# Samples' value pages summed by TensorE in strips of 32 columns, in batches of eight, instead of by VectorE

## The reference, cut to what matters

```
v_past = v_pool[page_table].reshape(db, past, HA, DVA)      # 8 samples x 2048 positions x 4 heads x 128
a = p[:, :, 0] - lam * p[:, :, 1]                           # weights of the two softmax maps
out = einsum('bhqk,bkhe->bqhe', a, v)                       # one query per sample
```

## Time and profile before

| | |
|---|---|
| time, median of 3 | 2703.87 us (2702.91 to 2704.54) |
| the profiled execution's own time | 2701.74 us, of which the span of the trace is 2699.8 us |
| TensorE busy | 2622.1 us, 97% of the span |
| VectorE busy | 1614.7 us, 60% |
| ScalarE, GpSimd busy | 1142.6 us, 1346.6 us |
| chunk loop | 572.30 to 770.13 us of the span |
| output projection | 766.82 to about 897 us |

### The profile page before, as it was taken

The page is one execution under the profiler, slowest core; times in us unless marked ns, Lnnn a source line. Parts: engine busy times, 40 slices in busy tenths (PEclk is TensorE's granted clock), DMA queues, the critical chain, the costliest instruction groups (busy, mean ns, idle before and its releaser), DMA issues.

```text
span 2699.8 us, 46857 instructions
## 1 busy us (share of the span) xinstructions
PE 2622.1 (97%) x17069; PEld 2408.8 (89%) x17069; DVE 1614.7 (60%) x3290; ACT 1142.6 (42%) x1771; POOL 1346.6 (50%) x613
## 2 busy tenths in 40 slices
PE   8999999978899999999999999999999999999998
PEld 5886666667766899999999999999999999999998
DVE  4227768889977343333337885378863788634323
ACT  2228739954423343334333434344343433444433
POOL 0210015610000666667666676676766767666663
PEclk9999999988899999999999999999999999999999
DMA  5220057634585444444444444454444444444553
GB/s 182 68 95 9 17 173 222 195 103 133 155 251 156 134 143 141 137 139 138 139 140 141 134 140 130 138 147 133 140 132 144 132 142 140 134 132 141 149 156 95
DMA packets 457194, 369.01 MB, mean 137 GB/s; under 512 B 15501, under 2 KB 400114, under 8 KB 456732
## 3 DMA queue, kind: packets, MB, share of 16 engines
q1 hardware_dynamic: 444846, 347.05, 43.6%
q0 software_dynamic: 2992, 12.26, 1.5%
q10 hardware_dynamic: 9174, 7.22, 0.9%
HBM read 351.17 MB, written 17.14 MB: 136 GB/s over the span
## 4 chain that ended last, share of the span: by engine, by line
PE 67%; DVE 2%; ACT 1%; issue 1%; DMA 0%; SPq 0%; POOL 0%; DVEq 0%; ACTq 0%
PE bank L2867 21%; PE bank L2869 21%; PE bank L2868 21%; PE bank L2359 3%; DVE tmp L2735 1%; DVE bank L3448 1%; ACT tmp L2727 1%; DMA big<-in_cache_attn_v 0%; PE bank L2743 0%; PE bank L3651 0%; PE bank L2379 0%; SPq L1128 0%; DVE hh L3405 0%; DVE hl L3406 0%; PE bank L1759 0%
## 5 line engine op out<-in xcount | busy, mean ns | idle before, releaser
L3326 POOL TENSOR_TENSOR wl<-wring,wh 128x1024 fp32r<-128x1024 f32 x466 | 1137.4, 2456 | 589.3 <-ACT wh L3083 588.9
L2867 PE MATMUL bank<-xh,wh 128*128 128x344 f32 x2688 | 862.2, 321 | 0.3 <-POOL wl L3326 0.3
L2869 PE MATMUL bank<-xh,wl 128*128 128x344 f32 x2688 | 858.4, 319 | 0.0
L2868 PE MATMUL bank<-xl,wh 128*128 128x344 f32 x2688 | 856.8, 319 | 0.0
L3083 ACT ACTIVATE wh<-wring 128x1024 fp32r<-128x1024 f32 x466 | 484.1, 1055 | 766.3 <-PE bank L2869 642.4
L2867 PEld LDWEIGHTS bank<-xh,wh 128*128 128x128 f32 x2688 | 505.6, 188 | 1.8 <-POOL wl L3326 0.6
L2868 PEld LDWEIGHTS bank<-xl,wh 128*128 128x128 f32 x2688 | 504.0, 188 | 1.2
L2869 PEld LDWEIGHTS bank<-xh,wl 128*128 128x128 f32 x2688 | 505.0, 188 | 0.0
L3404 DVE TENSOR_TENSOR bank<-bank,gates_tmp 128x344 f32<-128x344 f32 x132 | 69.1, 524 | 512.0 <-PE bank L2869 420.0
L3448 DVE SCALAR_TENSOR_TENSOR bank<-big,vec,bank 128x344 f32<-128x344 f32 (+1 forms) x696 | 354.5, 572 | 0.5
L2867 PE MATMUL bank<-hh,wh 128*128 128x344 f32 x1040 | 334.2, 321 | 3.2 <-DVE hl L3406 3.2
(11 more groups left out here) (441 smaller groups left out, 3182.9 us busy)
## 6 DMA issues: line engine op xcount, KB each, us to landing
wring<-in_ffn_w_down SPq DMA_DIRECT2D x132, 512.0 KB, 3.6
wring<-in_ffn_w_gate SPq DMA_DIRECT2D x131, 512.0 KB, 3.9
wring<-in_ffn_w_up SPq DMA_DIRECT2D x131, 512.0 KB, 3.9
wring<-in_conv_w_pw SPq DMA_DIRECT2D x72, 512.0 KB, 3.8
big<-in_cache_attn_k SPq DMA_DIRECT2D x128, 256.0 KB, 3.0
big<-in_cache_attn_v SPq DMA_DIRECT2D x128, 256.0 KB, 2.9
wring<-in_w_in SPq DMA_DIRECT2D x20, 512.0 KB, 4.0
park<-res_a SPq DMA_DIRECT2D x1, 4128.0 KB, 12.9
```

The lines of the kernel that those rows point to most:

```text
L2867: pe.matmul(bank_out, h, mh, start=(n == 0), stop=False)
L2868: pe.matmul(bank_out, h, ml, start=False, stop=False)
L2869: mm = pe.matmul(bank_out, l, mh, start=False, stop=(n == len(terms) - 1))
L3326: pool.tensor_tensor(wl[s % 6][:, :], raw_w[s % WQ] if raw is None else raw, wh[s % 6][:, :].bitcast(F32), ALU.subtract).then_inc(w_cut, 1)
```

## The change

96 of the 128 page sums move from VectorE to TensorE. Eight pages make a batch. `aw` holds the weights of a sample's pages side by side, four columns (heads) for a page, so a slice of 32 columns from a page's first on is taken as stationary operand: its first four columns are that page's heads, and the other 28 are results that nobody reads. The moving operand is the whole page, 128 x 512. Four such matmuls write four strips of 32 partitions of one PSUM bank, so a round of four takes two pairs of pages, a second round adds the next two pairs on top, and the batch is eight matmuls. VectorE then copies the bank to the accumulator (first half of a sample), or adds it (second half): one instruction of 128 x 512. In `page_column` a column of `fold` (ones at the partitions p with p mod 32 = h) replaces the column of ones.

```
-        PAGES = (0,) + 8 * (12,)
-        SAMPLE_AT = {2: 0, 4: 1, 5: 2, 6: 3, 8: 4}
+        BATCHES = (0, 1, 1, 2, 1, 2, 1, 2, 2)
+        SAMPLE_AT = {3: 0, 4: 1, 6: 2, 7: 3, 8: 4}
...
+        def page_batch(pe, k, t):
+            n = batch_bank(k, t)                 # bank 5, the second of an iteration bank 6
+            if k < NB:
+                pe.wait_ge((attn_done, k_scaled)[n - 5], k + 1)
...
+            for r in range(2):
+                for pp in (4 * half + 2 * r, 4 * half + 2 * r + 1):
+                    pe.wait_ge(page_in[pp % 4], b * 64 + 512 + 32 * (half + 1))
+                for q in range(4):
+                    pp, u = 4 * half + 2 * r + q // 2, q % 2
+                    at = (b * PG + 2 * pp + u) * H
+                    mm = pe.matmul(bank[32 * q:32 * (q + 1), n, :], aw_flat[:, at:at + 32], ring[:, pp % 4, u, :], start=(r == 0), stop=(r == 1))
+                mm.then_inc(vpage_used, 4)
+        def batch_copy(dve, k, t):
+            dve.wait_ge(vpage_used, 8 + 8 * (t + 1))
...
+                dve.tensor_tensor(d, d, src, ALU.add).then_inc(batch_in, 1)
...
+                dve.tensor_copy(d, src).then_inc(batch_in, 1)
...  chunk_pe
                 turn_keys(k)
+                for t in batches(k)[:1]:
+                    page_batch(pe, k, t)
                 left(k, 0)
...
                 right(k, 1)
+                for t in batches(k)[1:]:
+                    page_batch(pe, k, t)
...
                 right_turned(k, 1)
+                pe.wait_ge(batch_in, batches(k).start + 1)
                 values_new(k - 1)
                 left(k, 2)
+                pe.wait_ge(batch_in, batches(k).stop)
                 outputs(k - 1)
...  chunk_dve: page(k, 0) to page(k, 12) go
                 corrected(k - 1)
+                for t in batches(k)[:1]:
+                    batch_copy(dve, k, t)
...
                 join(k, 1)
+                for t in batches(k)[1:]:
+                    batch_copy(dve, k, t)
```

More of the change, by code:

```diff
@@ L1610, in build, with batches @@
         samp_full, sacc_done = sem("samp_full"), sem("sacc_done")
-        PAGES = (0,) + 8 * (12,)
-        LATE = sum(PAGES)
-        SAMPLE_AT = {2: 0, 4: 1, 5: 2, 6: 3, 8: 4}
+        BATCHES = (0, 1, 1, 2, 1, 2, 1, 2, 2)
+        LATE = 8 * sum(BATCHES)
+        SAMPLE_AT = {3: 0, 4: 1, 6: 2, 7: 3, 8: 4}
+        batch_in = sem("batch_in")
+        def batches(k):
+            return range(sum(BATCHES[:k]), sum(BATCHES[:k + 1]))
         KK, VT, QK, KT = 1, 2, 3, 4
@@ L1812, in page_column, with batch_bank @@
         def page_column(pe, b, n):
-            pe.wait_ge(vpage_used, 8 + PG * (b + 1))
+            if 2 * b < LATE // 8:
+                pe.wait_ge(batch_in, 2 * (b + 1))
+            else:
+                pe.wait_ge(vpage_used, 8 + PG * (b + 1))
             for h in range(H):
-                mm = pe.matmul(bank[:, n, h:h + 1], pacc[b][:, h, :], ones[:, 0:1], start=True, stop=True)
+                pick = fold[:, h:h + 1] if 2 * b < LATE // 8 else ones[:, 0:1]
+                mm = pe.matmul(bank[:, n, h:h + 1], pacc[b][:, h, :], pick, start=True, stop=True)
             mm.then_inc(samp_full, 1)
+        def batch_bank(k, t):
+            return 5 + (t - batches(k).start)
+        def page_batch(pe, k, t):
+            n = batch_bank(k, t)
+            if k < NB:
+                pe.wait_ge((attn_done, k_scaled)[n - 5], k + 1)
+            else:
+                pe.wait_ge((vn_copied, oc_copied)[n - 5], k - 1)
+            b, half = t // 2, t % 2
+            for r in range(2):
[7 more added lines that the diff above has]
+        def batch_copy(dve, k, t):
+            b, half = t // 2, t % 2
+            dve.wait_ge(vpage_used, 8 + 8 * (t + 1))
+            d, src = pacc[b].rearrange("p h e -> p (h e)"), bank[:, batch_bank(k, t), :]
+            if half:
+                dve.wait_ge(batch_in, t)
+                dve.tensor_tensor(d, d, src, ALU.add).then_inc(batch_in, 1)
+            else:
+                if b >= 2:
+                    dve.wait_ge(samp_full, b - 1)
+                dve.tensor_copy(d, src).then_inc(batch_in, 1)
         def page_column_in(dve, b, n):
@@ L2174, in chunk_dve @@
         def chunk_dve(dve, step):
-            def page(k, n):
-                if n < PAGES[k]:
-                    page_sum(dve, sum(PAGES[:k]) + n)
             def decays(c):
@@ L2297, in chunk_dve @@
             for k in range(1, NB + 1):
-                page(k, 0)
                 pairs(k)
                 join(k - 1, 3)
-                page(k, 1)
                 weights(k)
                 join_turned(k - 1, 3)
-                page(k, 2)
                 corrected(k - 1)
-                page(k, 3)
+                for t in batches(k)[:1]:
+                    batch_copy(dve, k, t)
                 join(k - 1, 4)
                 join(k, 0)
-                page(k, 4)
                 join_turned(k - 1, 4)
                 join_turned(k, 0)
-                page(k, 5)
-                page(k, 6)
                 join_turned(k - 1, 5)
@@ L2323, in chunk_dve @@
                 join(k, 1)
-                page(k, 7)
-                page(k, 8)
+                for t in batches(k)[1:]:
+                    batch_copy(dve, k, t)
                 join_turned(k, 1)
-                page(k, 9)
-                page(k, 10)
                 join(k, 2)
@@ L2331, in chunk_dve @@
                 join_turned(k, 2)
-                page(k, 11)
                 lower(k + 1)
-                page(k, 12)
                 if k in SAMPLE_AT:
```

## The result

| | before | after |
|---|---|---|
| time, median | 2703.72 us (2702.91 to 2704.54, 4 runs) | 2724.45 us (2722.45 to 2727.14, 4 runs) |
| ratio to before, with its 95% interval | | 1.0077 (1.006 to 1.0095) |
| profiled execution's own time, span | 2701.74, 2699.8 us | 2727.14, 2725.3 us |
| TensorE, VectorE busy | 2622.1, 1614.7 us | 2648.3, 1518.1 us |
| chunk loop, start to TensorE's first job of the projection | 572.30 to 766.82 | 574.12 to 791.47 |

The change is slower, as forecast, but by 20.7 us where 11.4 were forecast, and 0.4 us past the upper end of the range. VectorE is rid of 96.6 us of work and the kernel is slower nonetheless.

The account below looks back on a forecast made before the run. VectorE and TensorE taking turns in the chunk loop, neither full, were taken as the bound. -0.4 (k = 1 to 7), +3.8 (k = 8 and behind) and +8 (clock) gave +11.4, so 2713.1, 2715 as median; range 2700 to 2724.

Parts of the forecast that it names:

- Strips overlap: TensorE's batches: four 32-column strips run in the time of one; 0.90 us a round, 1.9 a batch with turn-over.
- The rival of serial strips: In the batches, strips do not overlap with 512 columns of pages: +64 us on top, 2779; chance 0.01.
- that of the turns: 24 turns between strip mode and whole array, at the 64 x 64 products, cost 0.5 us each: +12, 2727; chance 0.09.
- One iteration with one batch: Chunk-loop iteration with one batch at full clock: 22.15 us against 23.87 now; a sample's column adds 1.0.
- The second batch waits: In k = 3, 5, 7, 8 TensorE waits 3.4 us for pages; second round starts 13.3 us after first batch's start.
- the second batch does not wait: Two-batch iterations 24.05 us, k = 1 to 7 -10.6, k = 8 -1.5, 2692; chance 0.12 shared with better iterations.
- its two conditions: Either removes the second batch's wait: over 12 us between batches, or a page's issue under 0.8 us.
- The clock: Slow stretch behind each of the four second-batch waits: between nothing and 3.1 us each, 2.0 taken, +8 in all.
- the walk: Full-clock sum of loop stretches: k = 1 to 7 -0.4, k = 8 and behind +3.8, together +3.4 us.
- The clock holds: Rival: the chunk loop has no slow stretches behind its waits, +3.4 us, 2707; chance 0.24.
- k = 8 and `x_back`: Loop's end: fifth projection job 3.8 us later, the 1.46 us wait for an add goes, `x_back` near 780 us.
- What VectorE's pages cost before: In the chunk loop VectorE's pages cost about 2.5 to 3 us an iteration, not the 13.6 they occupy.

Follow-up runs that it names:

- iteration 3 without pages: The kernel before with the sums of the loop's 96 pages left out, loads and slot releases kept; 2670.02 us, ratio 0.9875.
- spaced: The changed kernel with its twelve whole batches spread evenly over the iterations, never two within one reload of the ring; 2690.78 us, ratio 0.9956.
- the filled kernel: The changed kernel with the first round of each second batch (k = 3, 5, 7, 8) done five times; 2712.62 us, ratio 1.003.
- the second form of the rounds: The changed kernel with three single rounds in each iteration instead of batches, plus page numbers read ahead; 2695.18 us, ratio 0.9964 (without reading ahead 2701.13 us).

## Why the prediction was off: point by point

**Strips overlap: right.** A round takes 0.93 us in the trace (two in the 1.85 us from 624.86 to the next product at 626.71), forecast 0.90 to 0.95. The rival of serial strips is out. So is that of the turns: the batch begins at 624.86, while the row before it still runs to 624.92, and the next product starts at 626.71, before the batch's modelled end. Iteration 2 with a batch takes 22.05 us and iteration 3 without pages 20.05 (neither has a column), so a batch with both its turns costs 2.0 us where its matmuls alone hold TensorE for 1.85. The Trainium skill says that changing the tiling mode drains TensorE (TensorEngine Tiling (Array Packing), Key Properties); the runs leave some 0.15 us for that and for everything else that a batch brings. The Trainium skill also has 2.38 times for three strips (TensorE: Matmul & The Clock Gate, Part 3), where four strips here again run in the time of one.

**One iteration with one batch: right where the clock holds.** 22.05 us (k = 2) and 23.17 (k = 4, with a column) against 22.15 and 23.15. In k = 1 (23.29) and k = 6 (24.57) the clock was at 0.94 and 0.93, which I had not forecast: +1.1 and +1.4. The prediction's sentence "In the other iterations TensorE is fuller than now and should stay at 1.00" failed there, and k = 6 shows its own sign of being wrong, an iteration with one batch over 24 us. In k = 1 the clock was as low before, and from the same source: a slow stretch that begins ahead of the loop (at 564.8 before, 566.6 now) and reaches 2.7 us into it in both.

**The second batch waits: right, and to 0.1 us.** The first round starts 8.7 us behind the first batch (forecast 8.9), the second at 13.38 (forecast 13.3), idle 3.64 (forecast 3.4), issues 1.20 us apart. The rival "the second batch does not wait" is out as the kernel stands. Of its two conditions one was right and one was not. With the batches over 12 us apart (spaced) the wait is nearly gone, and the time, 2690.8, is near what that rival gave (2692). With the issue under 0.8 us (0.52) a wait of 1.40 us stays, because the landings become the limit, and the time is 2704.3. The rival's "k = 8 gives -1.5" also does not follow from its terms: 4.3 + 10.8 + 1.0 + 5.0 + 23.6 = 44.7 against 44.3 is +0.4, so it should have said 2694.

**The clock: the step that failed.** The prediction put it so: "I expect a stretch at the low level behind each of the four ... I take 2.0, nearer to the trace's own slow stretch, as part of it may fall into the wait: +8." The stretches did come with each of the four, but the size is wrong. Two of them were longer than the 6.7 us that it was worked out from, and little of the four fell into the waits. Their lengths, in the windows of the trace at 0.50, were 6.8 us in k = 3 and 5, 10.2 in k = 7, 13.7 in k = 8:

```profile
638.30:645.10 6.80, 6.80 (x42) 4.79 (x44) 1.12 (x2) 0.05 (x1) 0.00 (x0) 0.50 0.74 213
692.90:699.70 6.80, 5.88 (x48) 3.87 (x48) 1.12 (x2) 0.60 (x1) 0.00 (x0) 0.50 0.78 219
...
747.50:757.70 10.20, 8.79 (x61) 6.68 (x62) 1.12 (x2) 1.50 (x6) 0.00 (x0) 0.50 0.99 295
778.20:791.90 13.70, 11.33 (x49) 9.34 (x50) 0.77 (x2) 1.20 (x2) 0.00 (x0) 0.50 0.67 206
```

In k = 3 the stretch begins as the wait ends. In the other three it begins before the wait's end (693.82, 748.91, 779.69), as these windows show, with TensorE idle and the clock already at 0.50:

```profile
692.95:693.80 0.85, 0.00 (x0) 0.01 (x1) 0.00 (x0) 0.00 (x0) 0.00 (x0) 0.50 0.78 207
747.55:748.90 1.35, 0.00 (x0) 0.02 (x1) 0.00 (x0) 0.00 (x0) 0.00 (x0) 0.50 1.03 313
778.30:779.65 1.35, 0.00 (x0) 0.00 (x0) 0.00 (x0) 0.00 (x0) 0.00 (x0) 0.50 0.86 281
```

So the allowance for a part in the wait was fair in kind, but it took off only 3.8 of 37.5 us (0.9, 1.4 and 1.5). The fill's recorded expectation, that the clock falls at the end of each wait, holds for k = 3 alone. The other 33.7 us lie on the chain, where TensorE does the second round, the column, `right_turned` and `values_new` at half speed, and in k = 8 the rest of the iteration. Beside the walk at the full clock (28.45, 27.45, 28.45 and 24.5 us) the four came out 3.6, 3.2, 4.4 and 4.3 longer, and the projection's start 0.6 longer, of which 0.4 is its wait for an add: 16.0 where 8 stood. The filled kernel takes 11.8 us of this back by the medians, and shows that it was the clock and not the wait's length; the rest, up to 16, is the walk's, and holds what it got wrong as well. The upper bound that I had, 3.1 us each, did not bound it: set against the filled kernel in the profiled executions, with the 0.1 to 0.4 us by which its second rounds start later, the four stretches cost 3.0, 2.3, 3.7 and 5.1 us. The bound came from the one slow stretch that I had looked at; the trace before has one of 10.2 us just ahead of and into the loop (clock 0.50 from 564.80 to 575.00). The range's upper end, 2724, held another 4 us for pages landing late. They landed on time, so the miss lies in the main with the clock's terms.

The account for the fifth job: forecast +11.4; clock behind the four waits +8.0; the clock in k = 6, +1.4; k = 1, +1.1; the loop's start in this execution +1.8; together 23.7, measured 23.8. By medians the start's 1.8 us need not be there, and 20.7 less 11.4 is 9.3, of which the clock behind the waits is the larger part.

**"The clock holds" (2707)** was wrong; but it is nearly the filled kernel's 2712.6, 5 us above. What remains, in its profiled execution, are k = 6 at a low clock (1.2 us), the filling's own delay (0.1 to 0.4 us in each of four), and three two-batch iterations that take some 0.6 us more than the walk says.

**k = 8 and `x_back`.** The fifth job was to start 3.8 us later against the state than before; in the filled kernel it starts 3.4 us later (797.88 - 750.22 = 47.7 against 44.3). That step holds, and the 1.46 us wait for an add became 0.37 in the changed one. `x_back` was issued at 793.01, not near 780: all that was lost in the loop, and the longer k = 8, lie ahead of it.

**What VectorE's pages cost before** I had at 2.5 to 3 us an iteration; it is 3.8. The sum did not hang on it, since the walk was built from the stretches, but a reader who set the change's worth by it would have called the prize 22 us instead of 33.7.

Not settled: what a lone round costs beyond the 1.00 us that it holds TensorE; what made k = 6 fall to the lower clock here (and k = 5 in the spaced kernel) while k = 2 and 4 didn't; why the stretches behind waits of 3.5 to 4.2 us are 6.8 us long in two cases and 10.2 and 13.7 in the others; and what kept the clock up in k = 8 of the second form of the rounds.

## What to carry to other kernels

A consumer that takes the whole ring at once needs a full reload (here 12.3 us from the first round's end to the last landing, for eight pages of 256 KB) before the next such bite, so place bites by that interval and not by iterations; the same twelve batches cost 20.7 us in one place and win 12.9 in another. A wait without work in TensorE's queue is to be priced with the slow stretch that follows it, nearly all of it on the chain: 2 to 5 us for a wait of 3.5 to 4.2 here. Harmless repeated matmuls in the wait are worth a try, as they took 11.8 us back. Price the slow stretch from the longest in the profile, not from one, and measure the prize of a change once by leaving the work out.

## What the runs showed of the hardware

- With each of the four waits of 3.5 to 4.2 us without work the granted clock fell to 0.50: in k = 3 as TensorE took up work again (clock at 638.30, work at 638.24), although it was 89% busy in the 8.7 us before the last round and its wait; in k = 5, 7 and 8 while it still stood idle, 0.9 to 1.5 us before the wait's end. It stayed there for 6.8, 6.8, 10.2 and 13.7 us with TensorE 83 to 100% busy. With the waits filled it stayed at 1.00 in all four iterations of the profiled execution.
- An issue of a page's DMA whose page number is read right before it takes 1.21 us; with the numbers already in registers it takes 0.52.
- Eight loads of 256 KB issued 0.52 us apart land about 1 us apart, with the DMA engines 96% busy at 335 GB/s; issued 1.21 us apart, the last of eight lands 2.9 us after its issue (635.21 to 638.10).
- Four float32 strips of 32 columns by 512 take 0.93 us together in a batch of two rounds, with no gap before or behind the batch against 64 x 64 and 128 x 128 products.
